# The last two experts in the order up, up, down, down, smaller first transfers and two fewer warm-up products in a one-core encoder block with 32 experts

## The reference

```python
h = rmsnorm(x, norm1_g)
z = h @ w_in                      # the latents are 416 of its columns
...
x = x + merged @ w_o
h2 = rmsnorm(x, norm2_g)          # 32 experts, 4 chosen for each token
gu = xblk @ w_gu[e] + b_gu[e]
gate = min(gu[:, :1024], 7); up = clip(gu[:, 1024:], -7, 7)
act = (up + 1) * (gate * sigmoid(1.702 * gate))
out[row_tok] += row_w * (act @ w_down[e] + b_down[e])
return rmsnorm(x + out, final_g)
```

## Time and profile before

| what | value |
|---|---|
| three runs, us | 1125.41, 1125.44, 1127.42; median 1125.44 |
| profiled execution, us | 1126.36 |
| its span, first to last instruction, us | 1124.5 |
| PE busy | 1089.8 us, 97% of the span |
| PE weight loads, DVE, ACT, POOL | 43%, 22%, 10%, 3% |
| HBM read | 433.66 MB, 387 GB/s over the span |
| mean granted TensorE clock | 0.992 |

### The profile page before, as it was taken

One profiled execution on the slowest core, in us unless ns is written; L12 is line 12 of the kernel. 1 busy time (PEld: TensorE's weight loads), 2 busy tenths in 40 slices (PEclk: granted clock), 3 DMA queues, 4 the chain that ended last, 5 costly groups with the idle time before them and its releaser, 6 DMA issues.

```text
span 1124.5 us, 12452 instructions
## 1 busy us (share of the span) xinstructions
PE 1089.8 (97%) x5272; PEld 481.3 (43%) x5273; DVE 246.5 (22%) x583; ACT 109.0 (10%) x244; POOL 29.2 (3%) x43
## 2 busy tenths in 40 slices
PE   9999999999999999999999999999999999999996
PEld 6758887534333333333333333333333333333321
DVE  3164212332121212121212221112121212121112
ACT  1152120300000000000000000000000000000002
POOL 2150000000000000000000000000000000000000
PEclk9999999999999999999999999999999999999999
DMA  9964376499999999999999999999999999999996
GB/s 361 397 239 169 112 279 249 162 366 422 416 423 434 430 431 430 429 434 432 434 432 431 429 434 429 436 430 434 430 429 434 432 434 432 431 423 428 421 421 260
DMA packets 30861, 435.14 MB, mean 387 GB/s; under 512 B 4528, under 2 KB 4784, under 8 KB 8560
## 3 DMA queue, kind: packets, MB, share of 16 engines
q1 hardware_dynamic: 29984, 432.76, 91.6%
q10 hardware_dynamic: 848, 1.97, 0.5%
HBM read 433.66 MB, written 1.05 MB: 387 GB/s over the span
## 4 chain that ended last, share of the span: by engine, by line
PE 66%; DMA 31%; DVE 2%; issue 0%; ACT 0%; SPq 0%; ACTq 0%; another core or an unknown queue 0%; DVEq 0%
DMA ring<-in_up 31%; PE ps L1568 27%; PE ps L1582 11%; PE ps L1383 5%; PE ps L1472 3%; PE ps L1590 3%; PE ps L1397 2%; PE ps L1456 2%; PE ps L1266 2%; PE ps L1577 2%; PE ps L1327 1%; PE ps L1253 1%; PE ps L1550 1%; PE ps L1544 1%; PE ps L1291 1%; DVE ring L885 1%
## 5 line engine op out<-in xcount | busy, mean ns | idle before, releaser
L1568 PE MATMUL ps<-ring,work 128*64 128x512 f32 x2044 | 469.8, 604 | 19.7 <-DMA ring<-in_up 19.3
L1568 PEld LDWEIGHTS ps<-ring,work 128*64 128x64 f32 x2044 | 140.7, 138 | 315.8 <-issue 276.3
L1582 PE MATMUL ps<-ring,work 128*64 128x512 f32 x1024 | 226.9, 595 | 0.8 <-DVE work L1159 0.8
L1043 DVE TENSOR_SCALAR work<-ps 128x512 f32<-128x512 f32 x32 | 22.1, 692 | 640.9 <-PE ps L1568 640.9
L1582 PEld LDWEIGHTS ps<-ring,work 128*64 128x64 f32 x1024 | 70.8, 137 | 133.2 <-issue 128.0
L1472 PEld LDWEIGHTS ps<-work 128*128 128x128 f32 x512 | 61.9, 191 | 22.5 <-issue 22.5
L1472 PE MATMUL ps<-work 128*128 128x128 f32 x512 | 70.2, 281 | 0.0
L1590 PE MATMUL ps<-work 64*128 64x512 f32 x264 | 65.6, 615 | 1.4 <-ACT work L723 0.7
L1383 PE MATMUL ps<-work,ring 128*128 128x256 f32 x256 | 56.6, 379 | 0.0
L1383 PEld LDWEIGHTS ps<-work,ring 128*128 128x128 f32 x256 | 48.6, 190 | 6.6
L697 ACT ACTIVATE work<-ps 128x256 f32<-128x256 f32 x33 | 12.6, 383 | 347.1 <-PE ps L1550 347.1
(11 more groups left out here) (181 smaller groups left out, 522.1 us busy)
## 6 DMA issues: line engine op xcount, KB each, us to landing
ring<-in_up SPq DMA_DIRECT2D x48, 4096.0 KB, 41.8
ring<-in_down SPq DMA_DIRECT2D x24, 4096.0 KB, 40.8
ring<-in_up SPq DMA_DIRECT2D x45, 1024.0 KB, 8.6
ring<-in_down SPq DMA_DIRECT2D x23, 1024.0 KB, 9.6
ring<-in_front SPq DMA_DIRECT2D x22, 1024.0 KB, 14.1
ring<-in_up SPq DMA_DIRECT2D x8, 2048.0 KB, 49.5
ring<-in_down SPq DMA_DIRECT2D x4, 2048.0 KB, 47.5
ring<-in_up SPq DMA_DIRECT2D x5, 512.0 KB, 4.4
```

The costliest lines, as they stand in the source:

```text
L1043: return dve.tensor_scalar(up_c, ps[:, UP, :], LIMIT, -LIMIT, ALU.min, ALU.max)
L1568: last = pe.matmul(ps[n * CAP:(n + 1) * CAP, bank, :], x, w[bank - GATE][:, n * BANK:(n + 1) * BANK], start=k == 0, stop=k == KT - 1, skip ...
L1582: done = pe.matmul(ps[n * CAP:(n + 1) * CAP, Y, :], lhs(actT, k), w[:, n * BANK:(n + 1) * BANK], start=first, stop=last, skip_group_check= ...
```

## The change

The start: x goes in four parts of 1, 1, 2 and 4 row blocks, the latents' weights in parts of 1, 1, 2, 2 and 2 row blocks. PE and DVE wait for the parts accordingly. Seven warm-up products rather than nine. On POOL the memset of the ones comes first.

The first pair: expert 0's turned activations go to `spare`, which is the space of the tokens `xT` that expert 0 has used up. DVE's clamp of expert 1's gate waits for the last up slot of expert 1 only (`pair_chain`). PE turns expert 1 before it scatters expert 0.

The last pair is written out in the manner of the first: up 30, scatter 29, up 31 with the turning of expert 30 within, down 30, turning of expert 31, down 31 with the scatter of expert 30 after its second slot. Expert 31's downs go to the bank MIX. The halved chain (`last_expert`) and the two halves of the last up slot are gone; turn 15 is loaded in the order in which it is used. The last down slot stays in halves.

```diff
+        spare = [xT[:, 0:n:n - 1].rearrange("p a k s -> p a (k s)") for n in (2, 3)]
...
-                a, z = ((0, COLS + 2 * SEQ), (COLS + 2 * SEQ, COLS + 4 * SEQ), (COLS + 4 * SEQ, COLS + 8 * SEQ))[n]
+                a, z = ((0, COLS + SEQ), (COLS + SEQ, COLS + 2 * SEQ), (COLS + 2 * SEQ, COLS + 4 * SEQ), (COLS + 4 * SEQ, COLS + 8 * SEQ))[n]
...
             x_part(0)
-            latent_half(0, 0, s_half[0])
+            latent_part(0, 0, 1, s_half[0])
             x_part(1)
-            latent_half(0, 1, loaded[0])
+            latent_part(0, 1, 1, s_half[1])
             x_part(2)
-            latent_half(1, 0, s_half[1])
+            latent_part(0, 2, 2, loaded[0])
+            x_part(3)
+            latent_part(1, 0, 2, s_half[2])
             for t in range(TT):
                 sp.dma_start(xrow[:, t:t + 1, :], x_rows[:, t:t + 1, :]).then_inc(s_x[t], 16)
-            latent_half(1, 1, loaded[1])
+            latent_part(1, 2, 2, loaded[1])
...
-            last_up = PER_EXPERT + UP_SLOTS - 1
-            for at in (*range(last_up), last_up, *range(last_up + 1, RING - 3), RING - 2, RING - 3):
...
+            for at in order[:RING - 1]:
+                fine_load(TURNS - 1, at)
...
+            pool.memset(all_ones, 1.0).then_inc(ones_set, 1)
             pool.memset(eps[:, :], -0.5).then_inc(zeroed, 1)
-            pool.memset(all_ones, 1.0).then_inc(ones_set, 1)
...
-            def last_expert():
...
+            def last_pair():
+
+                for u in range(PAIR):
+                    act.wait_ge(gT_done, E - PAIR + u + 1)
+                    take_gatedT(u).then_inc(gT_ready, 1)
+                    act.wait_ge(clamped, E - PAIR + u + 1)
+                    act.activation(sig, gate_c, ACT.Sigmoid, scale=ALPHA).then_inc(sig_ready, 1)
+                act.wait_ge(freed, N_FRONT + E * PER_EXPERT - DOWN_SLOTS)
+                act.activation(y_e, ps[:, Y, :], ACT.Copy).then_inc(y_ready, 1)
+                act.wait_ge(freed, N_FRONT + E * PER_EXPERT)
+                act.activation(y_e, ps[:, MIX, :], ACT.Copy).then_inc(y_ready, 1)
...
+            def pair_chain(e, base):
+
+                dve.wait_ge(up_done, e + 1)
+                clamp_up().then_inc(clamped2, 1)
+                dve.wait_ge(freed, base + UP_SLOTS)
+                clamp_gate().then_inc(clamped, 1)
+                raise_and_activate(e)
+                dve.wait_ge(actT_done, e + 1)
+
+            def spare_actT(pair):
+
+                dve.tensor_copy(spare[pair % 2], ps[:, MIX, :].rearrange("p (a n) -> p a n", a=2)).then_inc(actT_ready, 1)
...
+            def last_pair():
+
+                base = N_FRONT + (E - PAIR) * PER_EXPERT
+                pair_chain(E - 2, base)
+                spare_actT(1)
+                pair_chain(E - 1, base + UP_SLOTS)
+                dve.tensor_copy(actT, ps[:, MIX, :]).then_inc(actT_ready, 1)
...
-            for n in range(9):
+            for n in range(7):
                 pe.matmul(ps[:, 7, 0:P], all_ones, all_ones, start=True, stop=True)
...
-                first_down(0)
+                first_down(0, spare_lhs(0))
+                pe.wait_ge(gT_ready, 2)
+                pe.wait_ge(act_ready, 2)
+                turn(act_v).then_inc(actT_done, 1)
                 pe.wait_ge(y_ready, 2)
                 for n in range(2 * TT):
                     scatter(0, n)
-                pe.wait_ge(gT_ready, 2)
-                pe.wait_ge(act_ready, 2)
-                turn(act_v).then_inc(actT_done, 1)
...
+            def last_pair():
...
+                for u in range(PAIR):
+                    e = E - PAIR + u
+                    for k in range(KT):
+                        if u == 1 and k == 4:
+                            pe.wait_ge(gT_ready, e)
+                            pe.wait_ge(act_ready, e)
+                            turn(act_v).then_inc(actT_done, 1)
+                        up_tile(homes(pair, k // 4)[:, u, k % 4, :], k, last_weights(u * PER_EXPERT + k), up_done).then_inc(freed, 1)
+                        if k == 5:
+                            if u == 1:
+                                pe.wait_ge(actT_ready, e)
+                            pe.wait_ge(gated_ready, e + 1)
+                            turn_gated(u).then_inc(gT_done, 1)
+                        if k == 6:
+                            up_biases(u)
+                    if u == 0:
+                        pe.wait_ge(y_ready, e + 1)
+                        for n in range(2 * TT):
+                            scatter(1, n)
+                        pe.wait_ge(clamped2, e + 1)
+                        pe.wait_ge(clamped, e + 1)
+                for j in range(DOWN_SLOTS):
+                    w = last_weights(UP_SLOTS + j)
+                    down_tile(2 * j, w[0], j == 0, False, spare_lhs(1))
+                    down_tile(2 * j + 1, w[1], False, j == DOWN_SLOTS - 1, spare_lhs(1)).then_inc(freed, 1)
+                pe.wait_ge(gT_ready, E)
+                pe.wait_ge(act_ready, E)
+                turn(act_v).then_inc(actT_done, 1)
+                pe.wait_ge(actT_ready, E)
+                for j in range(DOWN_SLOTS):
+                    at = PER_EXPERT + UP_SLOTS + j
+                    if j == DOWN_SLOTS - 1:
+                        pe.wait_ge(last_half, 16)
+                        w = halves(at)
+                    else:
+                        w = last_weights(at)
+                    down_tile(2 * j, w[0], j == 0, False, bank=MIX)
+                    if j == DOWN_SLOTS - 1:
+                        w = last_weights(at)
+                    down_tile(2 * j + 1, w[1], False, j == DOWN_SLOTS - 1, bank=MIX).then_inc(freed, 1)
+                    if j == 1:
+                        pe.wait_ge(y_ready, E)
+                        for n in range(2 * TT):
+                            scatter(0, n)
```

More of the change, by code:

```diff
@@ L701, in _ @@
             take_gatedT(1, Y).then_inc(y_ready, 1)
-            def last_expert():
-                for h in range(2):
-                    cols = slice(h * SEQ, (h + 1) * SEQ)
-                    act.wait_ge(last_clamped, h + 1)
-                    act.activation(sig[:, cols], gate_c[:, cols], ACT.Sigmoid, scale=ALPHA).then_inc(last_sig, 1)
-                act.wait_ge(last_turned, 1)
-                act.activation(actT[:, 0:SEQ], ps[:, MIX, 0:SEQ], ACT.Copy).then_inc(last_actT[0], 1)
-                act.wait_ge(freed, N_FRONT + E * PER_EXPERT)
-                act.activation(y_e, ps[:, Y, :], ACT.Copy).then_inc(y_ready, 1)
             def first_pair():
@@ L1560, in halves, with up_tile @@
                 return ring[:, at, 0:F], ring[:, at, F:2 * F]
-            def up_tile(x, k, w, up_sem, gate_loaded=None):
+            def up_tile(x, k, w, up_sem):
                 for bank in (UP, GATE):
-                    if bank == GATE and gate_loaded is not None:
-                        pe.wait_ge(*gate_loaded)
                     for n in range(2):
@@ L1578, in up_biases, with spare_lhs, down_tile @@
                               skip_group_check=True)
-            def down_tile(k, w, first, last):
+            def spare_lhs(pair):
+                return lambda k: spare[pair % 2][:, k % 4 // 2, k % 2 * P + k // 4 * CAP:k % 2 * P + (k // 4 + 1) * CAP]
+            def down_tile(k, w, first, last, act_of=lambda k: lhs(actT, k), bank=Y):
                 for n in range(2):
-                    done = pe.matmul(ps[n * CAP:(n + 1) * CAP, Y, :], lhs(actT, k), w[:, n * BANK:(n + 1) * BANK],
+                    done = pe.matmul(ps[n * CAP:(n + 1) * CAP, bank, :], act_of(k), w[:, n * BANK:(n + 1) * BANK],
                                      start=first, stop=last, skip_group_check=True)
@@ L1725, in experts @@
                         scatter(1 - b, n)
-                    if following:
-                        if b == 0:
-                            pe.wait_ge(pick_ready, i * (UNROLL // PAIR) + (pair + 3))
-                        pe.wait_ge(clamped2, e + 1)
-                        gather(4 * b)
+                    if b == 0:
+                        pe.wait_ge(pick_ready, i * (UNROLL // PAIR) + (pair + 3))
+                    pe.wait_ge(clamped2, e + 1)
+                    gather(4 * b)
                     pe.wait_ge(gT_ready, e + 1)
-                    if static and e == E - 1:
-                        last_expert(use)
-                        continue
                     pe.wait_ge(act_ready, e + 1)
                     turn(act_v).then_inc(actT_done, 1)
-                    if following:
-                        for k in range(4 * b + 1, 4 * b + 4):
-                            last = gather(k)
-                        last.then_inc(gathered, 1)
+                    for k in range(4 * b + 1, 4 * b + 4):
+                        last = gather(k)
+                    last.then_inc(gathered, 1)
                     pe.wait_ge(actT_ready, e + 1)
```

138 lines of the change are left out of this document (35 added, 103 removed).

## The result

The changed kernel took 1128.93 us (median of 20 runs, 1127.16 to 1131.02) and the kernel before, on the same chip, 1125.96 (median of 20, 1125.11 to 1129.38). The ratio is 1.002, with an interval of 1.0013 to 1.0027: about 2.25 us slower (the medians lie 2.97 apart), where 0.87 was forecast; 1128.93 lies above the range given. The profiled execution took 1128.69 us with a span of 1126.9.

What follows compares the result with a forecast made beforehand. TensorE's pace was to bound the kernel until about 290 us, then DMA until the last landing, then TensorE behind it. Terms -0.49 (first pair), +0.1 (start), +1.26 (tail) gave +0.87 on 1125.44, so 1126.3 us; range 1123.6 to 1128.1.

Steps and rivals of the forecast that it cites:

- The bound: Whole kernel: TensorE's pace decides until about 290 us, then DMA at some 430 GB/s, then TensorE behind the last landing.
- T: End of the kernel: the last landing of weights; a microsecond TensorE gains before 289 us was to bring it a microsecond earlier.
- First pair: 240 to 290 us: expert 1's turn falls into TensorE's idle time, all that follows 0.49 us earlier; bounds 0 to -0.7.
- The last pair: End of the kernel: path behind expert 30's last down slot 11.22 us, so +1.26 us; bounds 0 to +1.9.
- The start: First 18 us: first product about 1.5 us earlier gains 0 to 0.1; taken as +0.1 us, between -0.3 and +0.7.
- price of the rows from the saturated stage: Start: sixteen more rows on each DMA engine cost 0.13 us, priced from 1 MB loads against four-slot loads.
- D: Rival, start: TensorE at half clock beyond 13.4 us delays the diagonal products, +5.7 us at most; 1128.1 at 17 us; chance 0.13.
- E: Rival, start: a fixed cost for each transfer puts the identity later, +4 us, 1130.2; chance 0.03.
- B: Rival, start: the identity lands earlier behind small first transfers, up to -1.6 us, 1124.7; chance 0.12.
- C: Rival, end of the kernel: the tail is not charged, -0.4 us, 1125.0; chance 0.15.
- F: Rival, last pair: TensorE falls behind in up 31 already, +0.5 us, 1126.8; chance 0.03.
- What was to be seen: Diagonals near 18.1 after over 1 us idle; turn 2 issued 0.5 earlier; no last half-slot wait; 0.9 us gap before expert 31's downs.

Runs made afterwards that it cites:

- gap filled: Kernel before with the new start plus four products of ones before TensorE's wait for the diagonals, result unread; 1127.69 us, ratio 1.0007.

## Why the prediction was wrong, point by point

**The bound** held. DMA is full from 290 us on, and T moves with the first issue of turn 2: from that issue to the landing of the last half slot it is 823.3 to 823.9 us in 15 of 18 profiles, of all versions. In three it is 824.4 or 824.5, all three among the six with the new last pair. I don't put this down to the new order: in these three the 16 DMA engines finish one load 4.2 us or more apart, and they do so by 1041 us, before the last turn's first load lands near 1055, in one of them at 888 us already. But no run was made that settles it. The start's 1.6 us of earlier work came to nothing for the reason given: the identity's landing.

**First pair**, -0.49: right in mechanism and 0.10 too large. The gathers do start 0.49 us earlier (0.48 in the part alone), but the weight loads of the gathers used to start 0.10 us ahead of their first product (271.22 and 271.32), behind the turn, and behind the scatter they start with it (both 271.87). What reaches the issue of turn 2 is -0.39 in all eight profiles.

**The last pair**, +1.26: right. The path from the last slot of expert 30 to the last half slot took 11.39 us instead of the forecast 11.22 (1114.86 - 1103.47), the down products end 1.3 us later behind the last landing, and the part alone costs 1.25 us in the mean. From the landing of the last half slot to the end of the span it is 13.2 to 13.5 us in the four profiles with this last pair and 11.5 to 12.2 in the twelve with the old one, 1.5 apart in the mean. The single wait for the turned rows (0.78 us idle) and the scatter were its named terms, and moving the scatter gave back 1.1.

**The start**, "I take +0.1 us": this is the step that failed. Over the three kernels with small parts and the identity in its old place (start alone, nine warm-up products, gap filled; 35 executions) the mean span is 1126.36 (standard error 0.22) against 1125.08 (0.12): +1.3 us, beyond even the upper bound of +0.7. With what was measured of the other two, the sum is -0.39 + 1.3 + 1.25 = +2.2, and that is the result. The term was mis-sized in two ways.

First, the landing of the identity. Here is the first operation of the mean squares in the second profile of the kernel before (large parts), and in the changed kernel run again (small parts):

```profile
14.57 0.69 DVE L815 CUSTOM_DVE_ANT_0 ring<-ring 128x512 f32<-128x512 f32 x1 [3.88 <-DMA const<-in_table]
```

```profile
15.73 0.69 DVE L806 CUSTOM_DVE_ANT_0 ring<-ring 128x512 f32<-128x512 f32 x1 [4.13 <-DMA const<-in_table]
```

With the large parts it starts at 14.34 (first pair alone), 14.64 (last pair alone), 14.47 (seven warm-up products), 14.57 and, in the earlier trace rows, 15.40; with the small parts at 14.99, 15.10, 15.19, 15.26, 15.30, 15.43, 15.72 and 15.73. The means are 14.68 over five profiles and 15.34 over eight: 0.66 us later, about the delay behind the upper bound of the prediction (+0.7, short rows a quarter slower) and five times its price of the rows from the saturated stage (0.13). And the profile on which the prediction rested had the latest identity of its five. Against it the changed kernel's 14.99 even looks like a gain of 0.4. In two profiles the small parts seem harmless, in thirteen they don't.

What the prediction left out of its price shows in a stretch of the start that it didn't use, 6 to 8 us, in the kernel before and then with the new start alone:

```profile
6.00:8.00 2.00, 1.88 (x3) 1.17 (x4) 0.28 (x2) 0.00 (x0) 0.00 (x0) 1.00 0.99 362
```

```profile
6.00:8.00 2.00, 2.00 (x7) 0.99 (x5) 0.61 (x2) 0.00 (x0) 0.00 (x0) 1.00 0.88 293
```

The five profiles with large parts move 349 to 396 GB/s there at a DMA share of 0.95 to 1.03, the eight with small parts 251 to 331 at 0.73 to 0.95. So the premise that two more issues on SyncE are hidden "as long as DMA has work" is not safe: the two row tiles of x are issued from 4.47 us instead of 3.52 and the identity at 6.68 instead of 5.76, and DMA is no longer full. Whether the shorter rows or the later issues make the delay, no run separates, since each has both; that it is the short rows is argued only.

How much of the delay gets through? I compared the same operation of DVE, a copy that starts at 214.23 us in the first profile of the kernel before. In twelve of the thirteen profiles its place follows the identity's landing to 0.03 us, so from the start to 217 us nothing else differs. The thirteenth is the second profile of the kernel before:

```profile
17.03 0.29 DVE L823 TENSOR_SCALAR ring<-const,sums 128x128 f32<-128x128 f32 x1 [0.23 <-POOL sums L517]
17.88 0.61 PE L1250 MATMUL ps<-ring 128*128 128x128 f32 x4
```

There the diagonals are ready at 17.32 us, and TensorE comes to them only at 17.88: its records of the latents take 901 ns between 7.2 and 10 us, the lower level of its clock, and its own products decide. So the old start has two limits that lie close together, the identity and TensorE's pace, and an earlier identity helps only where the clock has risen. The mean place of that copy is 213.65 with the large parts and 214.19 with the small ones: 0.53 us of the 0.66 get through.

Second, some 0.7 us of the 1.3 are left (standard error 0.3). Sending the identity first takes 1.9 us off the new start and 1.4 off the old in the mean. The copy at 214 us moves by 1.13 in the three profiles with the new start; with the old start it stands at 212.69 in one profile and at 214.19 in the other, where TensorE's records of the latents again take 892 ns. A candidate for the rest is the fall of the clock at 222 to 224 us, at 1.4 us or more each: one more in every second execution would do. The mean granted clock, 0.9897 with the small parts against 0.9902 before, leaves room for some of it. But the fall came in three of these eight profiles with small parts and in three of the five with large ones, and filling the gap brought nothing back that can be told. This remains open.

**The rivals.** D (the start loses) had the right sign and the wrong mechanism: it needed TensorE at its lower level until 13.4 us. In all eleven profiles with the new start its records of the latents take 521 to 537 ns between 7.2 and 10 us, the full level; it was the large parts that still had 858, 901 and 892 there, in three of seven profiles. E, the fixed cost of each transfer, would have put the identity 4 us later; the runs show 0.66 for two more transfers. The Trainium skill (DMA: Bandwidth & Descriptors, Anatomy of one DMA) gives its about 2.0 us for a DMA of the gpsimd path, and these are SyncE's, so the runs don't test its figure. The start's chance of a loss should have come from its own bound of +0.7, not from the clock alone. B and C are out: neither did the identity land earlier, nor was the tail free. F is out too: in the changed kernel TensorE stands 0.55 us for DMA ahead of the last down slot of expert 30, so it had not fallen behind.

**What was to be seen** came at the end: no wait for the last half slot, and a gap of 0.78 us between turn and downs of expert 31. At the start it came in part: the diagonals at 17.45 + 0.29 = 17.7 rather than 18.1, TensorE idle for 0.95 rather than over 1 us. The first load of turn 2 was later instead of earlier, by the clock's fall at 223 us. None of the signs of being wrong appeared, though the forecast was: in this one profile the start's loss can't be seen, since the profile that it is held against has the latest identity of its five.

## What to carry to other kernels

Before a start is cut into smaller transfers, look for the transfer whose landing ends the last wait there, and move that one forward; here this gave 1.4 us, and the smaller parts cost 1.3 while their own target, the first product, came 1.6 us earlier for nothing. A price taken where DMA is saturated didn't hold where it is just filling up. Near a balanced end every wait of TensorE behind the last landings counts in full, and an order that was costed step by step from rows came out within 0.3 us. Where terms are below a microsecond, take several profiles of the kernel before: a single landing at the start moved by 1.1 us from one execution to the next (14.34 to 15.40), more than any term of the forecast but the tail.

## What the runs showed of the hardware

The granted clock fell to the lower level in the router stage, at 222 to 224 us, in 8 of 18 profiles, with the old start (first pair alone, last pair alone, seven warm-up products) as with the new, behind a stretch in which TensorE idles for short times between dependent steps. How long it idled there doesn't tell the executions apart by itself: it was busy for 4.61 of the six us ahead of the fall in the changed kernel's first profile, and for 4.60 in the kernel before, which kept its clock. It cost 1.4 to 1.6 us, once 3.1. The falls of the DMA-bound stage, three or more in every profile (between 690 and 990 us), cost nothing that can be seen: the last half slot lands 823.7 us behind the first issue of turn 2 in the profile with three of them and 823.7 in the first of the kernel before, with four. The fall at 222 us is the largest cause of scatter that I found between executions of one kernel.

The clock's rise at the start scatters too. The records of the latents between 7.2 and 10 us take 858 to 901 ns in three of the seven profiles with large parts and 512 to 549 in all others. That no profile with small parts has the slow ones may be chance.

Another cause of scatter is the end of the last load: the 16 DMA engines finish it 3.1 to 4.3 us apart, 3.4 in the kernel before and 4.2 in the second profile of the changed one, and TensorE waits for the last.
